# Forgetting-attention input projection: seven products of quarter blocks for eight

## The reference

```python
def fox_project(x, w_in, b_f):                  # x: 512 + 8 tokens, 1024 features
    h = x @ w_in                                # w_in: 1024 x (3 * 1024 + 16)
    q, k, v, fl = jnp.split(h, [D_MODEL, 2 * D_MODEL, 3 * D_MODEL], axis=-1)
    ...
    logf = jax.nn.log_sigmoid((fl + b_f).astype(jnp.float32))
```

## Time and profile before

| | us |
|---|---|
| runs of the kernel before | 1679.16, 1688.98, 1692.68 |
| their median | 1688.98 |
| the profiled execution's own time | 1700.66 |
| its span, first to last instruction | 1698.9 |
| TensorE matmuls busy in it | 1517.1 |
| VectorE busy | 465.6 |
| ScalarE busy | 352.8 |

### The profile page before, as it was taken

The page is one execution under the profiler, slowest core; times in us unless marked ns, Lnnn a source line. Parts: engine busy times, 40 slices in busy tenths (PEclk is TensorE's granted clock), DMA queues, the critical chain, the costliest instruction groups (busy, mean ns, idle before and its releaser), DMA issues.

```text
span 1698.9 us, 21745 instructions
## 1 busy us (share of the span) xinstructions
PE 1517.1 (89%) x8599; PEld 1009.6 (59%) x8599; DVE 465.6 (27%) x979; ACT 352.8 (21%) x834; POOL 227.2 (13%) x246
## 2 busy tenths in 40 slices
PE   7999999999958999999999988988999994979990
PEld 6888888865733333377888863346885582323330
DVE  1421335322461111120101023341523256111114
ACT  0111111131041111121100046551114113111110
POOL 0000000000003642133300000000000000344323
PEclk9999899999978999999999999898999996989995
DMA  7221323354167998885277776852426325889837
GB/s 290 72 69 53 106 100 132 142 195 175 56 242 271 394 399 338 326 242 220 82 246 282 267 283 214 299 200 99 157 91 232 116 74 231 350 358 367 341 125 163
DMA packets 84477, 356.70 MB, mean 210 GB/s; under 512 B 21785, under 2 KB 25401, under 8 KB 57745
## 3 DMA queue, kind: packets, MB, share of 16 engines
q1 hardware_dynamic: 50192, 270.18, 42.4%
q0 software_dynamic: 23584, 48.03, 9.3%
q10 hardware_dynamic: 10601, 37.10, 5.5%
HBM read 402.92 MB, written 33.11 MB: 257 GB/s over the span
## 4 chain that ended last, share of the span: by engine, by line
PE 77%; DMA 8%; DVE 6%; ACT 4%; issue 3%; SPq 1%; POOL 1%; ACTq 0%; POOLq 0%; DVEq 0%
PE PS L579 73%; DMA MKV<-in_moe_w_gu,OVR 3%; DMA TOK<-y_rows,SLOT 3%; DMA W<-in_fox_v 2%; PE PS L1072 2%; DVE EX L1153 1%; PE PS L624 1%; ACT BIG L1912 1%; PE PS L958 1%; SPq L473 1%; ACT BIG L1917 0%; ACT X L1711 0%; PE PS L1094 0%; DMA y_rows<-BIG 0%; DMA W<-in_ab_w_in 0%
## 5 line engine op out<-in xcount | busy, mean ns | idle before, releaser
L579 PE MATMUL PS<-X,W 128*128 128x260 f32 x1792 | 406.4, 386 | 13.0 <-DMA W<-in_ab_w_in 9.3
L579 PEld LDWEIGHTS PS<-X,W 128*128 128x128 f32 x1792 | 339.8, 191 | 69.4 <-issue 13.6
L579 PE MATMUL PS<-O,W 128*128 128x260 f32 x1024 | 230.6, 386 | 2.4 <-DVE O L1472 1.6
L579 PEld LDWEIGHTS PS<-O,W 128*128 128x128 f32 x1024 | 195.0, 191 | 37.6 <-issue 3.4
L1649 ACT ACTIVATE BIG<-PS 128x512 f32<-128x512 f32 (+2 forms) x168 | 77.8, 463 | 401.5 <-PE PS L579 292.7
L579 PE MATMUL PS<-W,BIG 128*64 128x512 f32 x512 | 117.2, 612 | 2.0 <-DVE BIG L1600 2.0
L2094 POOL TENSOR_TENSOR SM<-SM,O 128x5 f32<-128x5 f32 x2 | 0.4, 196 | 847.9 <-DVE SM L1550 847.9
L579 PE MATMUL PS<-MKV,BIG 128*64 128x512 f32 (+1 forms) x384 | 90.9, 523 | 1.0 <-ACT BIG L1649 1.0
L579 PE MATMUL PS<-W,TMP 128*16 128x512 f32 (+2 forms) x512 | 78.9, 588 | 13.7 <-DMA W<-in_fox_v 13.7
L1605 DVE SCALAR_TENSOR_TENSOR BIG<-BIG,SM,PS 128x256 f32<-128x256 f32 x32 | 15.4, 480 | 253.3 <-ACT BIG L1971 253.3
L579 PEld LDWEIGHTS PS<-W,BIG 128*64 128x64 f32 x512 | 36.8, 141 | 71.4 <-issue 71.4
(11 more groups left out here) (288 smaller groups left out, 1626.9 us busy)
## 6 DMA issues: line engine op xcount, KB each, us to landing
W<-in_moe_w_gu SPq DMA_DIRECT2D x64, 1024.0 KB, 11.0
TMP<-in_moe_w_down SPq DMA_DIRECT2D x32, 1024.0 KB, 9.9
W<-in_fox_kt SPq DMA_DIRECT2D x64, 512.0 KB, 5.3
W<-in_fox_v SPq DMA_DIRECT2D x64, 512.0 KB, 5.5
W<-in_mem_wkv SPq DMA_DIRECT2D x16, 1024.0 KB, 5.1
W<-in_mem_kt SPq DMA_DIRECT2D x16, 1024.0 KB, 9.3
W<-in_cache_mem_v SPq DMA_DIRECT2D x16, 1024.0 KB, 8.6
y_rows<-BIG ACTq DMA_DIRECT2D x32, 512.0 KB, 8.9
```

The lines of the kernel that those rows point to most:

```text
L579: return nc.tensor.matmul(out, lhsT, rhs, start=start, stop=stop, **kw)
```

## The change

Blocks 1 to 11 of `fox_in` are computed by Winograd's form of Strassen's scheme. A block's output is seen as 2 x 2 quarters (tile, half), its weights as quarters `a11`, `a12`, `a21`, `a22` (tile by upper or lower half of the 1024 features), and X as `X11`, `X12`, `X21`, `X22` (half of the features by half of the tokens). With

    TX1 = X12 - X11    TX2 = X22 - TX1    TX3 = X22 - X12    TX4 = X21 - TX2
    S1 = a21 + a22     S2 = S1 - a11      S3 = a11 - a21     S4 = a12 - S2
    P1 = a11 X11       U2 = P1 + S2 TX2   U3 = U2 + S3 TX3
    C11 = P1 + a12 X21             C12 = U2 + S1 TX1 + S4 X22
    C21 = U3 + a22 TX4             C22 = U3 + S1 TX1

there are seven products of four matmuls (inner size 512) in place of four groups of eight. `C11` is collected in bank 0 or 3 by turns, `C21` with U2 and U3 as partial sums in bank 1, `C12` and `C22` in bank 2. ScalarE copies P1 into SBUF and evacuates `C11`; VectorE makes the TX once, the S for each block (one block ahead), reads U2 and U3 out of bank 1 in the middle of its accumulation, and evacuates the other three outputs with an addition. The TX lie in `TOK` and `MKV`, the S, P1, U2 and U3 in `MKV`; VectorE and ScalarE therefore wait for the stores of `MKV` before they first write there. Block 0, the order of the loads and the positions of the hooks stay; in a block, position 4b follows the third product, 4b + 1 the fifth, 4b + 2 the sixth and 4b + 3 the seventh.

```diff
+    if kind == "seven":
+        return [(0, 0), (0, 1), (1, 0), (1, 1)] + [(2 * b + m, h) for b in range(1, tiles // 2) for m, h in ((0, 0), (1, 1), (1, 0), (0, 1))]
...
+    if name == "fox_in" and m >= 2:
+        return "A" if (m % 2, h) == (0, 0) else "V"
...
+            if name == "fox_in" and pos >= 4:
+                b = (3 * (pos // 4 % 2), 2, 1, 2)[pos % 4]
...
+        XT_ = view(TOK, 0, 3, 4, HALF)
+        TX1, TX2, TX3, TX4 = XT_[:, 0], XT_[:, 1], XT_[:, 2], view(MKV, 0, 4, HALF)
+        S1, S2, S3, S4 = [view(MKV, 4 * HALF + 512 * j, 4, P) for j in range(4)]
+        P1S, U2S, U3S = [view(MKV, 4 * HALF + 2048 + HALF * j, HALF) for j in range(3)]
...
+            def seven(b, hooks):
+                g0 = PROJ.start["fox_in"] + 4 * b
+                a11, a12, a21, a22 = quarters(b)
+                c0, c2, c1, _ = [bank(PROJ.bank[g0 + j])[:, 0:HALF] for j in range(4)]
+
+                def product(out, lhs, rhs, start):
+                    for k in range(4):
+                        last = mm(out, lhs[:, k, :], rhs[:, k, :], start and k == 0, k == 3, skip_group_check=True)
+                    return last
...
+                pe.wait_ge(*arrived(PROJ.block0["fox_in"] + b))
+                wait_evac(pe, PROJ.count[PROJ.prev[g0]])
+                product(c0, a11, X11, True).then_inc(S("seven_acc"), 1)
+                pe.wait_ge(S("seven_s"), 4 * b - 2)
+                wait_evac(pe, PROJ.count[PROJ.prev[g0 + 2]])
+                product(c1, S2, TX2, True).then_inc(S("seven_acc"), 1)
+                pe.wait_ge(S("seven_A"), b)
+                product(c0, a12, X21, False).then_inc(S("proj_acc"), 1)
+                after(4 * b)
+                pe.wait_ge(S("seven_s"), 4 * b - 1)
+                pe.wait_ge(S("seven_V"), 2 * b - 1)
+                product(c1, S3, TX3, False).then_inc(S("seven_acc"), 1)
+                wait_evac(pe, PROJ.count[PROJ.prev[g0 + 1]])
+                product(c2, S1, TX1, True).then_inc(S("proj_acc"), 1)
+                after(4 * b + 1)
+                pe.wait_ge(S("seven_V"), 2 * b)
+                product(c1, a22, TX4, False).then_inc(S("proj_acc"), 1)
+                after(4 * b + 2)
+                pe.wait_ge(S("seven_s"), 4 * b)
+                wait_evac(pe, PROJ.count[g0 + 1])
+                product(c2, S4, X22, False).then_inc(S("proj_acc"), 1)
+                after(4 * b + 3)
...
-                    proj("fox_in", X, lambda m, h, pos: None, {1: forget, 8: logf_rows, 36: new_logits, **{17 + 2 * i: lambda i=i: key_quad(i) for i in range(16)}})
+                    hooks = {1: forget, 8: logf_rows, 36: new_logits, **{17 + 2 * i: lambda i=i: key_quad(i) for i in range(16)}}
+                    proj("fox_in", X, lambda m, h, pos: None, hooks, until=4)
+                    for b in SEVEN:
+                        seven(b, hooks)
...
+                    link(V.tensor_tensor(TX1, X12, X11, ALU.subtract))
+                    link(V.tensor_tensor(TX2, X22, TX1, ALU.subtract))
+                    link(V.tensor_tensor(TX3, X22, X12, ALU.subtract))
+
+                    def weight_sum(b, j):
+                        a11, a12, a21, a22 = quarters(b)
+                        if j == 0:
+                            dve.wait_ge(*arrived(PROJ.block0["fox_in"] + b))
+                        elif j != 2:
+                            dve.wait_ge(S("seven_s"), 4 * b - (3 if j == 1 else 2))
+                        out, x, y, op = ((S1, a21, a22, ALU.add), (S2, S1, a11, ALU.subtract),
+                                         (S3, a11, a21, ALU.subtract), (S4, a12, S2, ALU.subtract))[j]
+                        V.tensor_tensor(out, x, y, op).then_inc(S("seven_s"), 1)
+
+                    def fourth():
+                        dve.wait_ge(S("st_mkv"), 32)
+                        link(V.tensor_tensor(TX4, X21, TX2, ALU.subtract))
+                        for j in range(4):
+                            weight_sum(1, j)
...
+                        dve.wait_ge(S("seven_acc"), 3 * b - 1)
+                        dve.wait_ge(S("seven_A"), b)
+                        if b > 1:
+                            wait_evac(dve, PROJ.count[g0 - 1])
+                        V.tensor_tensor(U2S, c1, P1S, ALU.add).then_inc(S("seven_V"), 1)
+                        after(4 * b)
+                        dve.wait_ge(S("seven_acc"), 3 * b)
+                        V.tensor_tensor(U3S, c1, P1S, ALU.add).then_inc(S("seven_V"), 1)
+                        dve.wait_ge(S("seven_V"), 2 * b)
+                        put(1, c2, U3S)
+                        after(4 * b + 1)
+                        if b + 1 in SEVEN:
+                            dve.wait_ge(S("seven_s"), 4 * b)
+                            for j in range(3):
+                                weight_sum(b + 1, j)
+                        put(2, c1, P1S)
+                        after(4 * b + 2)
+                        put(3, c2, U2S)
+                        if b + 1 in SEVEN:
+                            weight_sum(b + 1, 3)
+                        after(4 * b + 3)
...
+                    evac("fox_in", put_fox, hooks, until=4)
+                    fourth()
+                    for b in SEVEN:
+                        seven(b, hooks)
...
+                    evac("fox_in", put_fox, {1: forget}, until=4)
+                    act.wait_ge(S("st_mkv"), 32)
+                    for b in SEVEN:
+                        g0 = PROJ.start["fox_in"] + 4 * b
+                        act.wait_ge(S("seven_acc"), 3 * b - 2)
+                        if b > 1:
+                            wait_evac(act, PROJ.count[g0 - 2])
+                        copy(P1S, bank(PROJ.bank[g0])[:, 0:HALF]).then_inc(S("seven_A"), 1)
+                        if b == 1:
+                            forget_exp()
+                        put_out("fox_in", 4 * b, put_fox)
+                        if b == 2:
+                            forget_rows()
```

More of the change, by code:

```diff
@@ L32 @@
 PHASES = [("ab_in", 16, "wide"), ("kv0", 16, "mem"), ("ab_o", 8, "halved"), ("mq0", 8, "halved"), ("mo0", 8, "halved"),
[L33 removed]
+          ("kv1", 16, "mem"), ("fox_in", 24, "seven"), ("fox_o", 8, "halved"), ("mq1", 8, "halved"), ("mo1", 8, "halved")]
 def groups_of(kind, tiles):
+    if kind == "seven":
+        return [(0, 0), (0, 1), (1, 0), (1, 1)] + [(2 * b + m, h) for b in range(1, tiles // 2) for m, h in ((0, 0), (1, 1), (1, 0), (0, 1))]
     if kind == "wide":
@@ L408, in wait_tr, with quarters @@
                 eng.wait_ge(S("tr_" + e), c)
+        XT_ = view(TOK, 0, 3, 4, HALF)
+        TX1, TX2, TX3, TX4 = XT_[:, 0], XT_[:, 1], XT_[:, 2], view(MKV, 0, 4, HALF)
+        S1, S2, S3, S4 = [view(MKV, 4 * HALF + 512 * j, 4, P) for j in range(4)]
+        P1S, U2S, U3S = [view(MKV, 4 * HALF + 2048 + HALF * j, HALF) for j in range(3)]
+        X11, X12 = X[:, 0:4, 0:HALF], X[:, 0:4, HALF:T]
+        X21, X22 = X[:, 4:8, 0:HALF], X[:, 4:8, HALF:T]
+        SEVEN = range(1, 12)
+        def quarters(b):
+            w = Wl[PROJ.slot[PROJ.block0["fox_in"] + b]]
+            return w[:, 0:4, 0:P], w[:, 4:8, 0:P], w[:, 0:4, P:2 * P], w[:, 4:8, P:2 * P]
         block = ctx.enter_context(nc.Block())
@@ L601, in proj, with after @@
                         hooks[pos]()
+            def seven(b, hooks):
[6 more added lines that the diff above has]
+                    return last
+                def after(pos):
+                    if pos in hooks:
+                        hooks[pos]()
+                pe.wait_ge(*arrived(PROJ.block0["fox_in"] + b))
[20 more added lines that the diff above has]
+                after(4 * b + 3)
             done = [0]
@@ L1134, in link, with evac @@
                 dve.wait_ge(S("dve_step"), steps[0])
-            def evac(name, put, hooks={}):
-                for pos, (g, m, h) in enumerate(PROJ.groups(name)):
+            def evac(name, put, hooks={}, until=None):
+                for pos, (g, m, h) in list(enumerate(PROJ.groups(name)))[:until]:
                     if evac_engine(name, m, h) == "V":
@@ new lines, in fourth, with seven, put, after @@
+                    def fourth():
[3 more added lines that the diff above has]
+                            weight_sum(1, j)
+                    def seven(b, hooks):
+                        g0 = PROJ.start["fox_in"] + 4 * b
+                        c0, c2, c1, _ = [bank(PROJ.bank[g0 + j])[:, 0:HALF] for j in range(4)]
+                        def put(j, src, part):
+                            g, m, h = PROJ.groups("fox_in")[4 * b + j]
+                            dve.wait_ge(S("proj_acc"), g + 1)
+                            dst = HT_[:, m, h * HALF:(h + 1) * HALF] if m < 16 else TMP[:, m - 16, h * HALF:(h + 1) * HALF]
+                            V.tensor_tensor(dst, src, part, ALU.add).then_inc(S("proj_V"), 1)
+                        def after(pos):
+                            if pos in hooks:
+                                hooks[pos]()
+                        dve.wait_ge(S("seven_acc"), 3 * b - 1)
```

(18 more changed lines are left out.)

3 lines of the change are left out of this document (removed).

## The result

| us | before | after |
|---|---|---|
| median of 8 runs each | 1689.14 | 1674.81 |
| range of the runs | 1679.16 to 1692.68 | 1666.28 to 1676.53 |
| the profiled execution | 1700.66 | 1672.04 |
| stage, first product of `fox_in` to first transpose of `v` | 211.55 | 195.52 |

The ratio is 0.9911, 95% interval 0.9887 to 0.9936: 14.3 us faster, 10.8 to 19.1. The forecast was 18.7 us and 1670.3. The two profiled executions lie 28.6 us apart, but only 16.0 of that is in the stage; 5.6 lies ahead of it, where nothing was changed. So the stage is read from the traces and the whole from the medians.

What follows compares the result with a forecast made beforehand. TensorE's matmul issue was taken to bound `fox_in`: 19.3 us saved on products less 0.6 for the first block gives 18.7, from the median 1688.98 to 1670.3 us. The range was 1661 to 1684.

Steps and rivals of the forecast that it cites:

- What bounds the stage: `fox_in`: the stage ends when TensorE has issued its last matmul; work taken from TensorE there is time.
- the price of a product: `fox_in` matmuls: 0.4386 us each; 28 for 32 in blocks 1 to 11 saves 1.754 a block, 19.3 us.
- VectorE and the hand-offs: `fox_in` blocks: VectorE gets 5.1 us in 12.3; each hand-off is covered by a 1.75 us product, costed at nothing.
- The rival that exposes them: Blocks 1 to 11: one hand-off a block late by 0.65 us, gain 11.5, time 1677.5; chance 0.14.
- The first block: Block 1's P1 waits once for ScalarE's copy of block 0's last group from bank 3: 0.6 us.
- Boundaries: Three more product starts a block, 33 in all: taken as nothing, 1.4 us kept for the range.
- The queues: Loads on SyncE's queue: weights and key pages still land in time, key pages by 2.3 to 4.6 us.
- that rival: Key pages set the pace of blocks with two key quads: gain 6.4 us, time 1682.6; chance 0.10.
- the late start of the value pages: Behind the stage: key quad frees first value pages 3.5 us later, gain 15.2, time 1673.8; chance 0.09.
- The clock: Rival in `fox_in`: waits open gaps, granted clock falls to 0.86, stage 12 us slower, time 1701.0; chance 0.05.
- the sum: Whole kernel: 19.3 saved on products less 0.6 for the first block gives 18.7 us.
- the prediction's own signs: Right if 680 product records, one 0.6 us wait, stage 192 to 193 us; wrong if clock under 1.00 inside it.

Runs made afterwards that it cites:

- seven eighths: Kernel before, with the last 128 of 1024 features left out of the products in blocks 1 to 11: ratio 0.9873, stage 191.38 us.
- banks exchanged: Kernel after, with banks 0 and 3 exchanged for C11, so block 1 doesn't start in the bank of block 0's last group: 1674.21 us.
- sums twice: Kernel after, with each weight sum of VectorE done twice: 1671.92 us, stage 195.78.
- later loads: Kernel after, with the two loads of fox_o's first weights moved on SyncE's queue behind the two key quads that follow each: 1677.22 us.
- burst in four parts: Kernel after, with C11's banks exchanged and new_logits issued in quarters at positions 36, 38, 40 and 42: 1672.25 us, ratio 0.9908.
- after, once more: Kernel after, run again with nothing changed: 1677.0 us, stage 196.65.
- cover taken away: Kernel after, with TensorE's second and third product exchanged, so P1's copy and U2 are wanted at once: 1686.82 us, stage 212.34.
- both edits: Kernel after, with C11's banks exchanged and new_logits moved from position 36 to 44: 1664.08 us, ratio 0.9866.
- position 37: Kernel after, with new_logits moved from position 36 to 37, directly ahead of key quad 10: 1667.42 us, stage 194.81.
- queues emptied: Kernel after, with SyncE holding key quad 11 until new_logits is done: 1677.07 us in one run, stage 193.62.

## Why the prediction was right

**What bounds the stage, and the price of a product:** right. 88 records less alone, in the kernel with seven eighths, are 19.7 us by the traces for 19.3 predicted; the changed kernel has 680 records and periods of 12.27 and 16.41 us where 12.28 and 16.4 were worked out.

**VectorE and the hand-offs:** right. Sums take 681 to 692 ns (0.73 was taken with the gap between them), outputs 427 to 429; VectorE is 45.5 us busier, "some 50" was said. No hand-off is late, that of `forget_sums` in block 2 included: one piece of the chain runs from 820.79 for 108 us. The rival that exposes them was priced at 0.65 us each; bare, they cost 0.80. Its mechanism is real, but this order covers it.

**The first block:** right in mechanism. The wait shown is 0.57 of the 0.6 predicted; by the kernel with the banks exchanged it costs 0.79 in all.

**Boundaries:** costed at nothing, bound 1.4; the runs leave some 0.3 for 33 of them.

**The queues:** key pages land in at most 8.9 us where 7.5 was read, and TensorE never waits for them. So that rival falls, and so does the late start of the value pages: TensorE waits 12.3 us for them in four places after, 13.7 in six before. From the stage's end to the first product of the output projection it is 161.3 us after and 163.8 before, in one execution each, so nothing is seen to be given back there.

**The clock:** the rival was wrong in its place and nearly empty in size. It expected gaps from hand-offs; the one gap has another cause. It costs 1.79 us of half clock, and no stage-wide loss.

**The step that failed is the sum.** "19.3 - 0.6 = 18.7" has no term for `new_logits`, whose instructions the change leaves alone. In the kernel before there is one gap of 0.50 us, 5.4 us behind the burst; now there is one of 1.47 in it, with 1.79 of slow clock: 18.7 - 0.97 - 1.79 = 15.9, and the stage became 16.0 shorter. That this fits to 0.1 is in part luck: the records saved are worth 19.7 and not 19.3, the first block costs 0.79 and not 0.6, and 0.3 is left for the boundaries, which nearly cancel. By the prediction's own signs the stage had to be 192 to 193 us at clock 1.00; it is 195.5 at 0.99, which stands among the signs of being wrong. For the whole, 14.3 us with an interval of 10.8 to 19.1 holds both 16 and 18.7; the time of 1674.81 is 4.5 above the forecast, partly this, partly the median's own scatter. Taken alone that time lies nearer to two rivals (value pages 1673.8, hand-offs 1677.5) than to the forecast: it is the traces that turn them down.

## What to carry to other kernels

When the end is set by one engine's issue, count its records, find the spacing from what hangs on them, and check each hand-off for the product that covers it: here 0.80 us each when bare, nothing when covered, so the order decides whether the saving exists. After an engine has been made faster, look in the trace for "issue" gaps where bursts of tiny instructions meet full DMA queues, find the last packet of the instruction queue ahead of the gap in the DMA view, and spread or move such a burst. Measure the stage in the trace when the change is worth less than the executions scatter.

## What the hardware showed that was not expected

TensorE can stand still for 0.5 to 2.6 us with nothing to wait for that the profile shows as a wait. In six executions of the changed order with `new_logits` at position 36 (the kernel after three times, sums twice, later loads, banks exchanged) the gap came between the same two instructions, at 1.47 to 2.59 us, with DMA shares of 0.92 to 1.06. Two things belong to it: with the same burst and idle queues (share 0.00) it is absent, and with full queues and the burst in four parts, too, in one profiled execution each. With seven products but the burst elsewhere it was under 0.4, 0.88 or 1.04 us. The kernel before has a share of 0.96 just ahead of its burst and 0.72 in it, no gap there, and one of 0.50 us that starts 5.4 us behind it, where the share is 0.99.

What comes late can be seen. The DMA view also counts the packets that carry instructions. The kernel after has 69 of them on `q8`, 16 KB each, for 17022 matmul and weight load records of TensorE; that they are TensorE's is inferred from this count and from the times below. In its 3 us from 928 on, one lies among 320 packets of data:

```profile
q8 instruction: 69, 1.13, 0.3%
...
q1 hardware_dynamic: 320, 1.19, 99.1%
q8 instruction: 1, 0.02, 2.0%
```

The table has the last such packet ahead of each gap, or ahead of the burst or in its first part where there is no gap (us; found by narrowing the view's window).

| kernel | packet | burst starts | TensorE goes on | after the packet's end |
|---|---|---|---|---|
| after | 928.12 to 929.06 | 927.51 | 930.31 | 1.25 |
| after, once more | 930.39 to 931.38 | 928.92 | 932.85 | 1.47 |
| banks exchanged | 925.86 to 926.88 | 925.04 | 928.38 | 1.50 |
| cover taken away | 940.08 to 941.06 | 938.96 | 942.29 | 1.23 |
| both edits | 970.15 to 971.10 | 969.60 | 972.62 | 1.52 |
| position 37 | 927.53 to 928.48 | 927.65 | 929.77 | 1.29 |
| before | 948.00 to 950.17 | 944.56 | 951.75 | 1.58 |
| queues emptied | 928.11 to 929.09 | 929.94 | no gap | |
| burst in four parts | 922.77 to 923.73 | 922.14 | no gap | |
| seven eighths | 932.04 to 933.55 | 933.64 | no gap | |

In all ten executions with a gap (the other three are alike: 1.43, 1.24 and 1.40) TensorE goes on 1.23 to 1.58 us after such a packet has landed. In the six of position 36 the packet starts 0.56 to 1.47 us after the burst has started; with the same TensorE program and the queues emptied it starts 1.83 us ahead of the burst, as the last loads end, and the gap is gone. The kernel with seven eighths has no gap in spite of full queues (share 0.84 in the burst, 0.97 in the 5 us behind it): its packet has landed 0.09 us before the burst starts. With the burst in four parts the packet is late, too, 0.63 us behind the first part, but long matmuls follow and no gap shows. The place of the gap fits as well. Two products more ahead of the burst (position 37) put it 17 matmuls earlier in the burst (two products are 16), behind the 114th; one product less ahead of it (cover taken away) puts the gap behind the 139th matmul from the burst's start in place of the 131st, and a product is 8 matmul records. So TensorE stands still because its instructions come late: the burst of very short instructions uses up what is there, while the next packet is under way. That full queues are what holds up the packet's start rests on the one execution with them emptied; behind which data it stood, and why TensorE takes another 1.2 to 1.6 us once it has landed, stays open.

The granted clock fell to 1.2 GHz for some 3.4 us behind gaps of 1.04 to 2.59 us that followed the tiny matmuls. It stayed at 2.4 behind the 0.88 us of the kernel with both edits and behind 1.12 us in the kernel with bare hand-offs, where the gap came some records of a large product later. So the gap's length alone doesn't decide it.
